# Modulation products of a two-layer trunk on four column groups, twenty of the twenty-four slabs moved

## The reference

```python
mod = jax.nn.silu(cvec) @ P['w_mod'][l] + P['b_mod'][l]
mod = mod.reshape(cvec.shape[0], 1, N_MOD, D_MODEL)
h = rmsnorm(x, g[0]) * (1.0 + mod[:, :, 1]) + mod[:, :, 0]
m, ctx = token_mixers(h, l, P, hg_lower, cache)      # h @ w_in (1024 x 9216), three branches, w_br, w_o
x = x + mod[:, :, 2] * rmsnorm(m, g[1])
h = rmsnorm(x, g[2]) * (1.0 + mod[:, :, 4]) + mod[:, :, 3]
f = swiglu(...) on layer 0, moe(...) with 8 experts on layer 1
x = x + mod[:, :, 5] * rmsnorm(f, g[3])
```

## Time and profile before

| | us |
|---|---|
| three timed runs | 2015.32, 2017.97, 2020.06 (median 2017.97) |
| profiled execution, its span | 2017.5 |
| PE busy in it | 1838.1 (91%) |
| DVE busy | 1257.1 (62%) |
| ACT busy | 988.4 (49%) |
| line 893, all modulation products | 9.48 to 178.10 |
| first panel of layer 0 starts | 179.93 |
| dense feed-forward of layer 0 | 521.90 to about 706 |
| the experts of layer 1 | from about 1105 |

### The profile page before, as it was taken

How to read it: one execution, slowest core, us unless ns; L and a number is a source line. 1 busy time by engine, 2 the same in 40 slices (tenths; PEclk the granted TensorE clock), 3 DMA queues, 4 the chain that set the end, 5 groups by cost and what they waited for, 6 DMA issues and landing times.

```text
span 2017.5 us, 21065 instructions
## 1 busy us (share of the span) xinstructions
PE 1838.1 (91%) x8174; PEld 1421.4 (70%) x8175; DVE 1257.1 (62%) x1077; ACT 988.4 (49%) x929; POOL 126.1 (6%) x78
## 2 busy tenths in 40 slices
PE   8999999988699959999976898989898989898996
PEld 1225888876588848888865687878787878787773
DVE  1103558873444445579843686868686868696872
ACT  2102445333444354353332676767676767675751
POOL 1000203310000001013200000000000000000000
PEclk9999999998899969999977899999999999999998
DMA  9886454424244334544323597979797979797950
GB/s 401 293 305 250 167 198 167 156 105 158 114 188 188 125 115 167 198 167 159 134 94 146 195 348 307 368 277 375 278 374 272 374 278 375 275 378 267 359 209 21
DMA packets 55794, 470.21 MB, mean 233 GB/s; under 512 B 6352, under 2 KB 6400, under 8 KB 8496
## 3 DMA queue, kind: packets, MB, share of 16 engines
q1 hardware_dynamic: 52848, 458.25, 59.5%
q0 software_dynamic: 2880, 11.02, 1.3%
HBM read 465.05 MB, written 4.19 MB: 233 GB/s over the span
## 4 chain that ended last, share of the span: by engine, by line
PE 88%; DVE 4%; ACT 4%; issue 3%; DMA 0%; POOL 0%; POOLq 0%; ACTq 0%; DVEq 0%
PE ps L918 24%; PE ps L920 23%; PE ps L919 23%; PE ps L893 8%; ACT w_hi L705 2%; PE ps L1088 2%; PE ps L980 1%; PE ps L1310 1%; PE ps L1050 1%; DVE ring_lo L1603 1%; PE ps L912 1%; PE ps L960 1%; ACT ring_lo L694 0%; DMA ring<-in_w_mod 0%; ACT wide L621 0%
## 5 line engine op out<-in xcount | busy, mean ns | idle before, releaser
L1603 DVE TENSOR_TENSOR ring_lo<-ring,w_hi 128x2048 fp32r<-128x2048 f32 x297 | 679.9, 2292 | 232.1 <-ACT w_hi L705 232.1
L918 PE MATMUL ps<-ring_lo,h_hi 128*128 128x512 f32 x1520 | 610.5, 402 | 31.1 <-issue 25.1
L705 ACT ACTIVATE w_hi<-ring 128x2048 fp32r<-128x2048 f32 x297 | 568.0, 1913 | 107.0 <-PE ps L920 97.6
L918 PEld LDWEIGHTS ps<-ring_lo,h_hi 128*128 128x128 f32 x1520 | 289.4, 190 | 93.7 <-issue 34.0
L1542 DVE TENSOR_TENSOR ring_lo<-ring,ring_lo 128x2048 fp32r<-128x2048 f32 x76 | 182.6, 2405 | 267.0 <-ACT ring_lo L694 266.4
L920 PE MATMUL ps<-w_hi,h_hi 128*128 128x512 f32 x880 | 346.2, 393 | 0.0
L919 PE MATMUL ps<-w_hi,h_lo 128*128 128x512 f32 x880 | 345.7, 393 | 0.0
L694 ACT ACTIVATE ring_lo<-ring 128x2048 fp32r<-128x2048 f32 x92 | 176.1, 1916 | 325.8 <-PE ps L920 213.3
L920 PE MATMUL ps<-ring_lo,h_hi 128*128 128x512 f32 x640 | 251.8, 393 | 0.0
L919 PE MATMUL ps<-ring_lo,h_lo 128*128 128x512 f32 x640 | 251.7, 393 | 0.0
L918 PE MATMUL ps<-ring_lo,act_hi 128*128 128x512 f32 x440 | 181.9, 413 | 41.6 <-DVE ring_lo L1603 41.6
(11 more groups left out here) (263 smaller groups left out, 1489.9 us busy)
## 6 DMA issues: line engine op xcount, KB each, us to landing
ring<-in_w_ff SPq DMA_DIRECT2D x297, 1024.0 KB, 6.9
ring<-in_w_in SPq DMA_DIRECT2D x36, 2048.0 KB, 8.0
ring<-in_w_mod SPq DMA_DIRECT2D x24, 2048.0 KB, 8.1
ring<-in_w_br SPq DMA_DIRECT2D x6, 2048.0 KB, 7.8
ring<-in_w_o SPq DMA_DIRECT2D x4, 2048.0 KB, 8.0
out<-state_out POOLq DMA_DIRECT2D x4, 512.0 KB, 4.9
x_sb<-in_x POOLq DMA_DIRECT2D x1, 1024.0 KB, 26.8
state<-in_s_ret POOLq DMA_DIRECT2D x2, 512.0 KB, 22.3
```

Of the source, the lines that this page charges most:

```text
L705: A(w_hi[p], ring[i % SLOTS][:, p * UNIT:(p + 1) * UNIT], ACT.Copy).then_inc(hi_ready[p], 1)
L918: mm(out, a_hi, b_lo, start=start, stop=False, skip_group_check=True)
L1603: V.tensor_tensor(ring_lo[i % SLOTS][:, part], ring[i % SLOTS][:, part], w_hi[p].bitcast(F32), ALU.subtract)\
```

## The change

`modulate` and its two parts go. In their place:

- A product has a stationary side of 32 columns and writes 32 PSUM partitions: block k goes to column group k % 4 of the array, partitions 32q to 32q + 31 of one bank (`mod_blocks`). Each slab still has 8 fp32 products of 512 columns. The four partial sums of the groups are added when the rows are turned: `turn_mod` is now an fp32 product with `fold` (four identity blocks on top of each other) and no transpose.
- Only slabs 0 to 3 of layer 0 (rows 0 and 1) are multiplied ahead of the first panel, through the ring (`modulate_first`).
- Slabs 4 to 11 of each layer are multiplied between the halves of panels 0 to 7 (`modulate_mix`), loaded in two 1 MB units to `mod_w`; SP issues them behind the load of panel j + 1. Slabs 0 to 3 of layer 1 are multiplied in steps 2, 4, 6 and 8 of the dense feed-forward (`modulate_ffn`), loaded whole to `mod_wide`.
- Each of these 20 slabs writes a bank of its own time (4 or 6), and DVE copies or adds it to `mod_rows` (`add_mod`), between the two low parts of `ahead`. ACT's copies are gone. Each batch is then turned, read and made to `modc`: in panel 8 and in step 9.
- PE waits for `mod_added` ahead of each next slab and ahead of the pieces that write the same bank.
- Slabs sit in other ring slots in layer 0: `wo` 1 follows `wo` 0 with three skips behind.

```diff
...
 MOD_FIRST = 4
-MOD_TURNS = L * NSLAB_MOD // SLOTS
-MOD_SPLIT = -(-MOD_FIRST // SLOTS) * SLOTS
-MOD_GROUPS = [range(0, MOD_SPLIT), range(MOD_SPLIT, L * NSLAB_MOD)]
-COND_PAD = 2 * max(len(r) for r in MOD_GROUPS) - 2
+MOD_LATER = NSLAB_MOD - MOD_FIRST
+QUAD = 32
+COND_PAD = 2 * MOD_LATER - 2
+MOD_BATCHES = [(0, 0, MOD_FIRST), (0, MOD_FIRST, NSLAB_MOD), (1, 0, MOD_FIRST), (1, MOD_FIRST, NSLAB_MOD)]
+MIX_MOD_BANK = [4, 4, 4, 4, 6, 6, 4, 6]
+FFN_MOD_STEP = [2, 4, 6, 8]
+FFN_MOD_TURN = 9
...
     if l == 0:
-        slabs = [("mod", n // NSLAB_MOD, n % NSLAB_MOD) for n in range(L * NSLAB_MOD)]
+        slabs = [("mod", 0, n) for n in range(MOD_FIRST)]
...
             slabs.append(("br", l, BR_AFTER[j]))
-    return slabs + [("wo", l, 0), ("skip", l, 0), ("wo", l, 1)] + [("skip", l, 1)] * (l == L - 1)
+    if l == 0:
+        return slabs + [("wo", l, 0), ("wo", l, 1)] + [("skip", l, i) for i in range(3)]
+    return slabs + [("wo", l, 0), ("skip", l, 0), ("wo", l, 1), ("skip", l, 1)]
...
+        mod_w = [mod_w0, u2[:, 2 * D:4 * D]]
+        mod_wide = [u[:, 3 * D:7 * D], u[:, 7 * D:11 * D]]
...
+        def mod_count(l, n):
+            return NSLAB_MOD * l + n + 1
+        def mod_rows_count(l, n):
+            if l == 0:
+                return 1 if n < MOD_FIRST else n - MOD_FIRST + 2
+            return MOD_LATER + 2 + n
...
+            def mod_units(l, n):
+                if n > MOD_FIRST or l:
+                    sp.wait_ge(mod_done, mod_count(l, n) - 1)
+                if n == MOD_FIRST and l:
+                    sp.wait_ge(gu_done, NFS)
+                for b in range(2):
+                    src = w_mod[l * NSLAB_MOD + n][:, b * UNIT:(b + 1) * UNIT]
+                    sp.dma_start(mod_w[b], src).then_inc(mod_in, 16)
+            def mod_slab(n):
+                if n >= 2:
+                    sp.wait_ge(mod_done, mod_count(1, n - 2))
+                sp.dma_start(mod_wide[n % 2], w_mod[NSLAB_MOD + n]).then_inc(mod_wide_in[n % 2], 16)
             for l in range(L):
-                slabs = layer_slabs(l)
-                if l == 0:
-                    for s in range(SLOTS):
-                        load(slabs[s])
-                    with sp.Fori(1, MOD_TURNS) as t:
-                        for s in range(SLOTS):
-                            sp.wait_ge(mod_done, t * SLOTS + (s - SLOTS + 1))
-                            sp.dma_start(ring[s][:, 0:KD * 512], w_mod[t * SLOTS + s]).then_inc(slab_in[s], 16)
-                    slabs = slabs[MOD_TURNS * SLOTS:]
-                for key in slabs:
+                for key in layer_slabs(l):
...
                         load(key)
+                    if key[0] == "win" and 1 <= key[2] <= MOD_LATER:
+                        mod_units(l, MOD_FIRST + key[2] - 1)
...
                         load(("ffn", 0, i))
+                        if i + 1 in FFN_MOD_STEP:
+                            mod_slab(FFN_MOD_STEP.index(i + 1))
...
-            def modulate(part):
-                slabs = MOD_GROUPS[part]
-                height = 2 * len(slabs)
-                for i, n in enumerate(slabs):
-                    s, u, _ = plan[("mod", n // NSLAB_MOD, n % NSLAB_MOD)]
+            def mod_blocks(n, w, blocks, bank, start, stop):
+                at = COND_PAD - 2 * n
+                for k in blocks:
+                    q = k % 4
+                    ins = mm(ps[q * QUAD:(q + 1) * QUAD, bank, :], cond_pad[:, k, at:at + QUAD], w[:, k - blocks[0], :],
+                             start=start and k < 4, stop=stop and k >= KD - 4, skip_group_check=True)
+                return ins
+            def modulate_first():
+                for n in range(MOD_FIRST):
+                    s, u, _ = plan[("mod", 0, n)]
...
                     w = ring[s][:, 0:KD * 512].rearrange("p (k c) -> p k c", k=KD)
-                    at = COND_PAD - 2 * i
-                    for k in range(KD):
-                        ins = mm(ps[0:height, part, :], cond_pad[:, k, at:at + height], w[:, k, :],
-                                 start=(i == 0 and k == 0), stop=(n == slabs[-1] and k == KD - 1), skip_group_check=True)
-                    ins.then_inc(mod_done, 1)
-            def turn_mod(part):
-                height = 2 * len(MOD_GROUPS[part])
-                pe.wait_ge(mod_copied, part + 1)
+                    mod_blocks(n, w, range(KD), 0, n == 0, n == MOD_FIRST - 1).then_inc(mod_done, 1)
+            def modulate_mix(l, j):
+                if j:
+                    pe.wait_ge(mod_added, mod_rows_count(l, MOD_FIRST + j - 1))
+                if j == 4:
+                    pe.wait_ge(t_read_dve, 5 * l + 2)
+                if j == 6:
+                    pe.wait_ge(ro_read, l + 1)
+                if j == 7:
+                    pe.wait_ge(t_read_dve, 5 * l + 4)
+                pe.wait_ge(mod_in, 32 * (MOD_LATER * l + j + 1))
+                for b in range(2):
+                    w = mod_w[b].rearrange("p (k c) -> p k c", k=4)
+                    ins = mod_blocks(j, w, range(4 * b, 4 * b + 4), MIX_MOD_BANK[j], b == 0, b == 1)
+                ins.then_inc(mod_done, 1)
+            def modulate_ffn(n, i):
+                pe.wait_ge(actT_ready, i)
+                pe.wait_ge(mod_wide_in[n % 2], 16 * (n // 2 + 1))
+                w = mod_wide[n % 2].rearrange("p (k c) -> p k c", k=KD)
+                mod_blocks(n, w, range(KD), 6, True, True).then_inc(mod_done, 1)
+            def turn_mod(batch, bank):
+                l, first, end = MOD_BATCHES[batch]
+                width = 2 * (end - first)
+                pe.wait_ge(mod_added, mod_rows_count(l, end - 1))
                 for c in range(4):
-                    ins = nc.tensor.transpose(ps[:, 2 + part, c * height:(c + 1) * height],
-                                              mod_rows[0:height, part, c * P:(c + 1) * P], ident[0:height, 0:height])
+                    ins = mm(ps[:, bank, c * width:(c + 1) * width], mod_rows[:, c * P:(c + 1) * P], fold[:, 0:width],
+                             start=True, stop=True)
...
                     pe.wait_ge(mod_ready, l + 1)
-                    pe.wait_ge(mod_read, 1)
                 for half in range(2):
+                    if half and j < MOD_LATER:
+                        modulate_mix(l, j)
+                    if half and j == MOD_LATER:
+                        turn_mod(2 * l + 1, 6)
...
                     pe.wait_ge(rope_ready, 2 * l + q + 1)
+                if q == 2:
+                    pe.wait_ge(mod_added, mod_rows_count(l, MOD_FIRST + 5))
+                if q == 4:
+                    pe.wait_ge(mod_read, 2 * l + 2)
...
-            def ffn(tiles, base, acc_wait, before_last=None):
+            def ffn(tiles, base, acc_wait, before_last=None, mods=False):
...
                         pe.wait_ge(act_ready, base + i)
+                        if mods and i - 1 in FFN_MOD_STEP:
+                            pe.wait_ge(mod_added, mod_rows_count(1, FFN_MOD_STEP.index(i - 1)))
+                        if mods and i - 1 == FFN_MOD_TURN:
+                            pe.wait_ge(mod_read, 3)
...
                         for p, done in ((0, gua_done), (1, gu_done)):
+                            if mods and p and i in FFN_MOD_STEP:
+                                modulate_ffn(FFN_MOD_STEP.index(i), i)
+                            if mods and p and i == FFN_MOD_TURN:
+                                pe.wait_ge(actT_ready, i)
+                                turn_mod(2, 6)
...
-            pe.wait_ge(cond_ready, 1)
-            modulate(0)
+            pe.wait_ge(setup_act, 1)
+            modulate_first()
             turn_rows(0, 0)
-            turn_mod(0)
-            modulate(1)
-            turn_mod(1)
+            turn_mod(0, 2)
...
+            folded = 2 * MOD_LATER
+            link(V.tensor_tensor(fold, ident[:, 0:folded], ident[:, QUAD:QUAD + folded], ALU.add))
+            for q in (2, 3):
+                link(V.tensor_tensor(fold, fold, ident[:, q * QUAD:q * QUAD + folded], ALU.add))
...
-            def read_mod(part):
-                slabs = MOD_GROUPS[part]
-                dve.wait_ge(mod_turned, part + 1)
-                return V.tensor_copy(mod_raw[:, 8 * slabs[0]:8 * slabs[-1] + 8].rearrange("p (n c g) -> p n c g", c=4, g=2),
-                                     ps[:, 2 + part, 0:8 * len(slabs)].rearrange("p (c n g) -> p n c g", c=4, g=2))
-            def modulation(l, first, end, raw, done, value):
+            def add_mod(l, n, bank):
+                dve.wait_ge(mod_done, mod_count(l, n))
+                at = mod_rows_count(l, n)
+                batch = 2 * l + (n >= MOD_FIRST)
+                if batch == 0 or n == MOD_BATCHES[batch][1]:
+                    if batch:
+                        dve.wait_ge(mod_turned, batch)
+                    ins = V.tensor_copy(mod_rows, ps[:, bank, :])
+                else:
+                    dve.wait_ge(mod_added, at - 1)
```

(71 more changed lines are left out.)

50 lines of the change are left out of this document (25 added, 25 removed).

## The result

The change made the kernel faster: 1945.13 us (median of 4 runs, 1943.53 to 1946.83) against 2017.42 (4 runs, 2015.32 to 2020.06) on the same chip. The ratio is 0.964, with a 95% interval of 0.962 to 0.965. The forecast was 1988: a gain of 29 us where 72 came. The profiled execution took 1944.42 us for a span of 1942.6.

What follows compares the result with a forecast made beforehand. PE was taken as the bound, fully busy in the panels and feed-forward steps. 2017.5 - 116.0 (start) + 86.7 (moved slabs, turns, turnings) = 1988.2 us for the span; forecast 1988, range for 8 in 10 1942 to 2012.

Steps and rivals of the forecast that it cites:

- The direction: Whole kernel: faster, at a chance of 0.77; slower 0.22, within 0.2% 0.01.
- the gain of the start: Ahead of the first panel: four slabs instead of 24, panel at 61.2 us in place of 179.93, gain 116.0 us.
- the price of a moved slab: Slabs inside panels and feed-forward: 3.86 us each, 77.2 us for 20, bounds 36 and 137.2.
- The step that failed: Narrow products of a moved slab on PE: strict order lets records run only in pairs, 9 steps, 3.86 us.
- three turnings of rows: Inside the panels and the feed-forward, on PE: 8 records each at 0.12 us, 2.9 us in all.
- panel 5: DVE's adding behind the retention's output: hidden with pairs; with 1.8 us per slab PE waits 1 us, in both layers.
- The likeliest case: Moved slabs: records run in pairs on the column groups, 3.86 us a slab, 1988 us; chance 0.50.
- the rival with full concurrency: Moved slabs: all four groups stream side by side, 1.8 us a slab, 1949.5 us; chance 0.25.
- The half-clock products at its head: Head of the first panel: some 13 products at half clock behind PE's idle stretch, 2.7 us lost.
- The insertion's own cost: Each insertion in a panel or step: two turns between full and narrow products, 0.165 us each, 6.6 us for 20.
- Late data or adding: Panels with moved slabs: some of 16 wait for units, 3 us each, 48 in all, 2036 us; chance 0.05.

Runs made afterwards that it cites:

- the first experiment: Changed kernel with block k on column group k // 2 in place of k % 4, so neighbouring products share a group: 1947.07 us, ratio 0.965.
- the last two experiments: Changed kernel with layer 0's decay tables moved behind the first splits: 1936.84 us; the same with `level_mask` also loaded behind `x`: 1927.88 us.

## Why the prediction was off

The direction and the gain of the start were right; the price of a moved slab was put at twice what it is, because PE was taken to start its records strictly in order.

- **The step that failed** is "If PE starts matmuls strictly in order, the second record of k waits for the first, and only the first of k + 1 can join it: pairs, 17/2 rounded up, 9 steps of 0.429, 3.86 us." The runs showed 4 rounds and 1.85 us in the trace; the kernel with neighbours on one group shows why: a record behind others of another group does not wait for them. The support given in the forecast ("no row shows one overtaking") was empty: the rows of before hold only products that share columns with their neighbours, so they could not have shown one. The rule of the Trainium skill, TensorE: Matmul & The Clock Gate, Part 3 (Packing small matmuls), that matmuls keep program order in start and end does not hold for the products of the first experiment, taken in the order of the program (that they reach PE in this order is argued there, not shown). The other rule cited from there holds in kind: of four records side by side, each starts about 7 ns behind the last here, where it gives some 4.
- **Its size.** An insertion was put at 3.86 + 0.33 = 4.19 us and measured 2.05. Over 20 of them that is 20 x 2.14 = 42.8 us. With every term as measured the sum is 2017.5 - 115.2 (start) + 41.0 (20 insertions) + 2.7 (three turnings of rows at 0.91 us) + 1.6 (panel 5, both layers) - 3.1 (routing) = 1944.5, beside a span of 1942.6; 1.9 us stay open. The likeliest case fell and the rival with full concurrency, 1949.5, came. Its 1.8 us a slab, from 16 weight loads behind each other, is near 1.85 by chance: eight of these loads, 0.11 us each, lie within 0.16 us in the trace, so they don't add up. What a slab costs is four rounds and the return to full width.
- **The start** was right to 1 us, in part because two small errors offset each other. Panel 0 came at 62.73, not 61.2: the constants landed 1.7 us later (27.58 against 25.84), perhaps because of the denser loads, which no run separates. The half-clock products at its head cost about 2.0 us, not 2.7. The gain is 117.2 - 2.0 = 115.2 us against 116.0. The forecast did not see that the start could be shorter still (the last two experiments).
- **The insertion's own cost** was right: 0.33 forecast, 0.32 to 0.35 measured. That the array drains when the tiling mode changes (the Trainium skill, TensorEngine Tiling (Array Packing), Key Properties) agrees with a price, and the price is small. No run separates it from other causes of the same 0.17 us a turn.
- **Late data or adding:** right. The units land 5.0 and 7.1 us after issue and no product waits. Panel 5 has its 0.8 us wait in each layer, as the forecast gave for a short slab (1 us):

```profile
mod_w<-in_w_mod SPq DMA_DIRECT2D x16, 1024.0 KB, 5.0
u<-in_w_mod SPq DMA_DIRECT2D x16, 1024.0 KB, 7.1
```
```profile
150.77 1.06 PE L1009 MATMUL ps<-con,wide 128*128 128x128 f32 x8 [0.78 <-issue]
```

(That row names no releaser. The wait is put down to DVE's reading of the bank because it is where and about as long as that was worked out to be, and because it goes as the forecast said when PE comes there later: 0.4 us where half of the slab came later, none with two groups, where the slab takes 3.56 us.)
- **Not foreseen:** 3.1 us from a clock that rose earlier in the routing of layer 1. No run ties it to the change; it is luck.

## What to carry to other kernels

Products that use a quarter of the array's columns can be put on the four column groups, and their time falls by the number of groups, also where one fp32 product is two records and where neighbours in the program share a group. Don't leave such work at the start, where loads bound it: cheap products pay best where PE is the bound and DMA has room, and the two changes have to be judged together. When a block of work leaves the start, look again at everything it covered: tables and loads that stood beside it unnoticed were worth some 17 us here.

## What was not expected of the hardware

- Records of different column groups overtake each other, if they reach PE in the order of the program: with products 0 to 3 on groups 0 and 1 and products 4 to 7 on groups 2 and 3, records of 0 to 3 and of 4 to 7 started within 0.04 us of each other, and six records of 0 to 3 started behind the first of 4 to 7.
- The scaling is whole: 6.99, 3.56 and 1.85 us for 16 records on one, two and four groups. The weight loads (about 0.11 us each) run side by side as well: the first eight of a slab lie within 0.16 us.
- Eight narrow records of 0.6 us each stand in a merged row of PE's timeline as 1.04 to 1.06 us. A record's duration is not its cost; the distance between the full-width neighbours is.
- The same 32 products behind a wait of 1.69 to 1.73 us took 4.89 to 6.97 us in nine kernels, by the moment at which the granted clock rose. Which of these a kernel gets could not be told from its changes.
